# Order of small matmuls in the RWKV-7 mixer of a two-layer hybrid trunk

## The reference

```python
def step(state, inp):
    r_t, w_t, k_t, v_t, kk_t, b_t = inp
    sa = -jnp.einsum('bhvk,bhk->bhv', state, kk_t)
    state = state * w_t[:, :, None, :] + sa[..., None] * b_t[:, :, None, :] + v_t[..., None] * k_t[:, :, None, :]
    return state, jnp.einsum('bhvk,bhk->bhv', state, r_t)
```

## Time and profile before

| | |
|---|---|
| median of 3 executions | 2127.91 us (2127.08 to 2136.88) |
| profiled execution | 2126.94 us, of which the span is 2125.1 us |
| mean granted TensorE clock | 0.973 of full speed |
| busy share: TensorE matmul, weight load | 94%, 72% |
| busy share: VectorE, ScalarE, GpSimd | 65%, 52%, 5% |
| HBM read | 480 MB, 226 GB/s over the span |

### The profile page before, as it was taken

One profiled execution on the slowest core, in us unless ns is written; L12 is line 12 of the kernel. 1 busy time (PEld: TensorE's weight loads), 2 busy tenths in 40 slices (PEclk: granted clock), 3 DMA queues, 4 the chain that ended last, 5 costly groups with the idle time before them and its releaser, 6 DMA issues.

```text
span 2125.1 us, 23988 instructions
## 1 busy us (share of the span) xinstructions
PE 2000.5 (94%) x9114; PEld 1532.6 (72%) x9114; DVE 1377.9 (65%) x1377; ACT 1111.0 (52%) x1089; POOL 103.9 (5%) x124
## 2 busy tenths in 40 slices
PE   6999999989989989999789999999999999999997
PEld 5856666468877756665468788887878878788786
DVE  4672444335445753344169888888888888888886
ACT  4465111144334554111157677777767777776774
POOL 1340000000000520000000000000000000000000
PEclk9999998999999999998989999999999999999999
DMA  9533021444446432032089898998989989899993
GB/s 328 169 119 110 10 119 40 166 171 165 179 161 203 139 119 79 1 119 80 11 293 365 324 345 333 346 364 317 365 325 352 358 325 369 325 347 351 329 375 145
DMA packets 181490, 485.66 MB, mean 229 GB/s; under 512 B 5880, under 2 KB 12660, under 8 KB 172600
## 3 DMA queue, kind: packets, MB, share of 16 engines
q1 hardware_dynamic: 176256, 475.53, 61.1%
q0 software_dynamic: 1488, 5.57, 0.8%
q10 hardware_dynamic: 3688, 3.74, 0.7%
HBM read 480.06 MB, written 1.05 MB: 226 GB/s over the span
## 4 chain that ended last, share of the span: by engine, by line
PE 85%; DVE 6%; ACT 4%; issue 2%; POOL 1%; DMA 1%; ACTq 0%; DVEq 0%; SPq 0%
PE bank L1431 40%; PE bank L1011 17%; PE bank L1003 7%; PE bank L1111 6%; PE bank L1401 1%; PE bank L1385 1%; PE bank L1462 1%; DVE w_lo L1492 1%; PE bank L1215 1%; ACT w_hi L939 1%; PE bank L1295 1%; DMA ring<-moe_w_gate_dram 1%; DVE xg_lo L1919 1%; PE bank L1228 1%; DVE xterm L1492 1%
## 5 line engine op out<-in xcount | busy, mean ns | idle before, releaser
L1492 DVE TENSOR_TENSOR w_lo<-ring,w_hi 128x2048 fp32r<-128x2048 f32 x336 | 764.1, 2290 | 153.1 <-ACT w_hi L939 153.1
L939 ACT ACTIVATE w_hi<-ring 128x2048 fp32r<-128x2048 f32 x336 | 643.6, 1916 | 159.2 <-PE bank L1431 158.0
L1431 PE MATMUL bank<-w_hi,xg_hi 128*128 128x512 f32 x896 | 354.2, 395 | 9.2 <-DVE w_lo L1492 9.2
L1431 PE MATMUL bank<-w_hi,xg_lo 128*128 128x512 f32 x896 | 350.5, 391 | 0.0
L1431 PE MATMUL bank<-w_lo,xg_hi 128*128 128x512 f32 x896 | 350.4, 391 | 0.0
L1431 PEld LDWEIGHTS bank<-w_hi,xg_hi 128*128 128x128 f32 x896 | 169.5, 189 | 44.5 <-DVE w_lo L1492 10.4
L1431 PEld LDWEIGHTS bank<-w_hi,xg_lo 128*128 128x128 f32 x896 | 168.7, 188 | 35.6
L1431 PEld LDWEIGHTS bank<-w_lo,xg_hi 128*128 128x128 f32 x896 | 168.9, 189 | 34.1
L1431 PE MATMUL bank<-w_hi,ehT_hi 128*128 128x512 f32 x448 | 176.9, 395 | 3.6 <-DVE w_lo L1492 3.6
L1111 PE MATMUL bank<-ring,hnT 128*128 128x512 f32 x384 | 175.9, 599 | 0.0
L1431 PE MATMUL bank<-w_lo,ehT_hi 128*128 128x512 f32 x448 | 174.6, 390 | 0.0
(11 more groups left out here) (385 smaller groups left out, 2745.1 us busy)
## 6 DMA issues: line engine op xcount, KB each, us to landing
ring<-moe_w_gate_dram SPq DMA_DIRECT2D x56, 2048.0 KB, 7.8
ring<-moe_w_up_dram SPq DMA_DIRECT2D x56, 2048.0 KB, 8.4
ring<-moe_w_down_dram SPq DMA_DIRECT2D x56, 2048.0 KB, 7.9
ring<-w_in_dram SPq DMA_DIRECT2D x26, 2048.0 KB, 8.5
ring<-w_branch_dram SPq DMA_DIRECT2D x6, 2048.0 KB, 11.5
ring<-ffn_w_gate_dram SPq DMA_DIRECT2D x5, 2048.0 KB, 8.1
ring<-ffn_w_up_dram SPq DMA_DIRECT2D x5, 2048.0 KB, 8.1
ring<-ffn_w_down_dram SPq DMA_DIRECT2D x5, 2048.0 KB, 7.6
```

Source lines behind the costliest of these rows:

```text
L939: A.activation(w_hi[:, q % PARTS, :], ring[:, i, o:o + HALF], ACT.Copy).then_inc(s.hi_ready, 1)
L1431: ins = M(dst, a, w, start=start and n == 0, stop=stop and n == 2, skip_group_check=True)
L1492: return V.tensor_tensor(out_, a, b, op)
```

## The change

In the pair products the two heads of one `hp`, one in each half of the rows, take turns: first matmul of e = 0, first of e = 1, second of e = 0, second of e = 1. Both banks are asked for ahead of the four matmuls. The list of jobs and VectorE's masks follow the new order (heads 0, 4, 1, 5, 2, 6, 3, 7). In Y all matmuls with 128 rows of one `e` come first, then those with 64 rows, by chunk. Start flags are set on the first matmul of a bank alone. The arithmetic and the number of instructions are the same.

```diff
+PAIRED = [4 * e + hp for hp in range(4) for e in range(2)]
...
-        out += [(f"M{t}{i}", V) for i in range(NH)]
+        out += [(f"M{t}{i}", V) for i in PAIRED]
...
-                for i in range(NH):
-                    e, hp = i // 4, i % 4
-                    half = slice(64 * e, 64 * e + 64)
-                    if e == 0:
-                        read_out(pe, f"kT{t}{hp}.{l}")
-                    b = bank(f"M{t}{i}.{l}")
-                    M(b[:, 0:256], tT[half, hp, 256:384], tT[half, hp, 0:256], start=True, stop=True)
-                    done(M(b[:, 256:512], tT[half, hp, 384:512], tT[half, hp, 0:256], start=True, stop=True))
+                for hp in range(4):
+                    read_out(pe, f"kT{t}{hp}.{l}")
+                    bs = [bank(f"M{t}{4 * e + hp}.{l}") for e in range(2)]
+                    for c in range(2):
+                        for e, b in enumerate(bs):
+                            half = slice(64 * e, 64 * e + 64)
+                            ins = M(b[:, 256 * c:256 * c + 256], tT[half, hp, 256 + 128 * c:384 + 128 * c],
+                                    tT[half, hp, 0:256], start=True, stop=True)
+                            if c:
+                                done(ins)
...
-                        M(b[:, dst], m1[:, 4 * e + hp, 384:512], vcol[:, hh], start=True, stop=False)
-                        for n in (2 * t, 2 * t + 1):
-                            if n:
-                                o = 64 * (n % 2)
-                                M(b[o:o + 64, dst], tT[half, hp, 128 + o:192 + o], st[half, n - 1, hp, :],
-                                  start=False, stop=False)
-                        ins = M(b[:, dst], m1[:, 4 * e + hp, 128:256], uu[:, t, hh], start=False, stop=True)
+                        M(b[:, dst], m1[:, 4 * e + hp, 384:512], vcol[:, hh], start=hp == 0, stop=False,
+                          skip_group_check=True)
+                        ins = M(b[:, dst], m1[:, 4 * e + hp, 128:256], uu[:, t, hh], start=False, stop=hp == 3,
+                                skip_group_check=True)
+                    for n in (2 * t, 2 * t + 1):
+                        for hp in range(4 if n else 0):
+                            o = 64 * (n % 2)
+                            ins = M(b[o:o + 64, 64 * hp:64 * hp + 64], tT[half, hp, 128 + o:192 + o],
+                                    st[half, n - 1, hp, :], start=False, stop=True, skip_group_check=True)
...
-                for i in range(NH):
+                for i in PAIRED:
                     b = product(dve, f"M{t}{i}.{l}")
                     free(tt(m1[:, i, :], b[:], C("pair_mask"), ALU.mult), f"M{t}{i}.{l}")
```

## The result

The changed kernel takes 2101.47 us (median of 4, 2100.93 to 2109.03). The ratio to the kernel before, timed on the same chip, is 0.9837, with a 95% interval of 0.9812 to 0.9862. A second set of executions gave 0.9847 (0.9827 to 0.9867), 2101.6 against 2139.8 us. So the kernel is 1.6% faster, about 34 us; forecast were 18 us.

What follows compares the result with a forecast made beforehand. TensorE was taken to bound both changed places. Pair products 10.4 us plus Y 7.2 made 17.6, off the profiled 2126.94: 2109.3, with 1.0 for the median 2110 us (+- 3, 45%); range 2098 to 2119.

Steps and rivals of the forecast that it cites:

- What bounds the kernel: Pair products up to `B`, and Y: TensorE ends last in both, so what it saves there is saved at the end.
- Part 1: Pair products: heads in different row halves overlap, a stage takes 3.75 us instead of 6.35; four stages gain 10.4 us.
- The cover: Pair products: VectorE's masks, 0.61 us apart, stay hidden behind TensorE, with 5.7 us of slack left at `B`.
- Part 2: Products of Y: grouping leaves 4 tile changes a block instead of 16; four stages take 32.5 instead of 39.7 us, gain 7.2.
- The slack of `y_rwkv`: Behind Y of block 1: VectorE finishes normalising 6.5 us before TensorE wants the result, and this slack stays.
- I assume first that it falls as long after the stage's start as now: Y: the clock falls from 2.4 to 1.2 GHz as long after the stage's start as before; gain 7.2 us.
- rival B: Y of block 0: the clock stays up there, in one or both layers; kernel at 2103 to 2107 us; 30%.
- the median of the runs shown stands 1.0 us higher: Whole kernel: 1.0 us added to the 2109.3 us reckoned from the profiled execution of 2126.94, giving 2110.
- D: Only half works: the pair products gain no more than now (2120 us) or Y gains nothing (2117); 15%.
- E: Pair products: each turn between row halves costs 0.14 us and passes don't overlap; kernel slower at 2132 us; 4%.
- The rule weighed against the grouping: Y: a weight load overlaps running matmuls only if row groups differ, so 16 whole-array passes would each wait for theirs.
- C: Y of block 1: the clock stays up there as well, some 12 us in all, kernel at 2092 us; 6%.

Runs made afterwards that it cites:

- before_again: Unchanged copy of the kernel before, run and profiled again: 2141.3 us (2128.56 to 2144.6).
- y_twice: Changed kernel with the products of each Y bank issued twice, the second set over the first: 2132.7 us, ratio 0.9957.
- y_only: Kernel before with only the products of Y grouped, pair products as before: 2120.1 us, ratio 0.9911.
- pairs_only: Kernel before with only the new pair products, Y as before: 2124.6 us, ratio 0.9935.
- quads: Changed kernel with the 64-row products of Y taking turns over row halves and chunks, those of dU over the halves: 2106.0 us, ratio 0.9819.
- early_v: Changed kernel with the products of `m1` and `v` of block 1 issued ahead of the two waits before Y: 2103.4 us, ratio 0.983.
- heads: Changed kernel with both matmuls of e = 0, then both of e = 1, instead of turns matmul by matmul: 2102.3 us, ratio 0.985.
- all_edits: Changed kernel plus `quads`, `early_v` and the down projection begun ahead of the last transposes in the expert loop: 2075.3 us, ratio 0.9702.

## Why the prediction was off

*What bounds the kernel* was right: TensorE ends the chain in both places, and what it saved there (25.6 us by the stages) was saved at the end (25.4 us).

*Part 1* was right in mechanism. Forecast were stages of 3.75 us and 10.4 us in all; measured 3.63 to 3.68 and 11.2. The cover held: VectorE's masks fell to 0.60 apart, and `B` has 5.7 us of slack, as was said. But one term was mis-sized: the 6.79 us of layer 1, block 1 were counted "as the others", at a gain of 2.6; it was 3.1 between the first profiles, and `before_again` took 12.44 us there, 5.6 more.

*Part 2, at a given clock,* was right to a few hundredths in block 0: 5.07 us against 5.1. In block 1 the stages took 8.94 and 9.13 us against 9.6 and 9.0. The slack of `y_rwkv` is 5.7 us and not 6.5: ready at 356.7, wanted at 362.4. The 7.2 us given for the old block 1 at full speed are too high, since one `hp` takes some 0.85 us there too, which makes 6.8; nothing in the sum uses them.

*The step that failed* is "I assume first that it falls as long after the stage's start as now". It does not fall in block 0 at all. That was rival B with 30%, priced at up to 6.6 us for both layers; measured, Y of block 0 and its transposes give 12.0 us against 5.3 in the sum (2.5 and 2.8 for the stages), so 6.7 us. The argument against B, that the fall came early enough to lie inside the shorter stage too, took the fall for a matter of time since the stage began. `y_twice` shows it is not. The rows could not decide it: Z, the same shape in a row, stands there at full clock, but is over in 2.0 us, before the earliest fall in Y. That the old Y had 16 changes of tile in a block, and small products between the large ones, was known; that the clock hung on the order was not.

*The second failed step* is "the median of the runs shown stands 1.0 us higher": the sum was made against a profiled execution that was itself an exception. 2127.9 was taken for the kernel's time, and it is 2139.8. The remaining 9 to 13 us of the measured gain fit falls of the clock in the expert loop and in the pair products, which one of the two profiles of the kernel before shows and neither of the changed kernel's does, but for one fall; that most executions of the kernel before have them is argued from their times. The 5.6 us in the pair products are the change's own, as they carry on the fall in Y. The loop is not touched by the change, and `y_only`, `pairs_only`, `quads` and `early_v`, which reach it 3 to 18 us earlier or later than the changed kernel, show four to six falls in their profiles. So I put that part of the gain down to when the loop begins and not to what the change does; this is argued, and what decides whether an execution has the falls stays open.

*Rivals.* D and E are out: the one overlap of before was not special, and a turn costs nothing (3.66 us a stage with 15 turns, 3.76 with 7 in `heads`). The rule weighed against the grouping does not hold here: 16 whole-array passes in a row stand 0.11 apart with their weight loads beside them. C was right to be small: in block 1 the clock falls some 1.5 us into Y in both layers (8.94 us at 0.59, 9.13 at 0.58), much as before, and `early_v` shows that it does so even with the longer of the two waits filled. Only `all_edits` comes near C, with a mean clock of 0.92 where the changed kernel has 0.69.

## What to carry to other kernels

A TensorE stage that is busy for its whole length can still be half empty: look at the rows and columns of its matmuls, and put neighbours into different halves of the array or sort them by shape, which saves the changes of tile and in block 0 kept the clock up here. When the granted clock of the stage that you change is between its two levels, price both levels and do not assume that the fall stays where it was. And take several profiles of the kernel before ahead of the sum: a wait of under 2 us in a loop was worth 1.9 us a pass by itself (128.0 to 126.1), and another 1.5 (129.5) in executions in which the clock fell at it.

## What the runs showed of the hardware

Passes in different halves of the rows run side by side even when four passes of one half are queued ahead of the first of the other (`heads`: 3.76 us for 32 passes of 0.216). Passes in different quarters do so too, as far as they were tried (`quads`: 32 small passes, spread by turns over the four quarters, in 1.06 us at half speed, where the changed kernel takes 1.53 for each 16, one quarter after the other). Ten microseconds of Y in groups, 16 passes with 128 rows and then 8 with 64, held 2.4 GHz (`y_twice`), while the same passes mixed two by two did not the earlier trace rows; and the groups of block 1, which began at 1.2 GHz, stayed there for 21 us. Pair products on one half of the rows held the clock where they began with it. Where they began without, it came back 1 us into them in one execution (6.79 us at 0.93) and not at all in another (`before_again`, 12.44 us at 0.50). A fall of the clock can repeat at one place of a loop for six passes in a row (`before_again`) and be absent from all passes of another execution of the same kernel (the first profile).
